# Down projection of three chunks by seven products, with one weight sum per pair made by an accumulating transfer and three by VectorE

## The chip, the core and the metric

The kernel runs on one core of a Trainium2 chip. The metric is the device time of one execution in microseconds (us), as the median of three runs. The profile is one further execution, recorded by the hardware profiler. Engines are called as the profile calls them: PE is TensorE's matmul, DVE is VectorE, ACT is ScalarE, POOL is GpSimd, SP is SyncE, which only issues transfers.

## What is computed

One inference step of an encoder layer over 512 prompt tokens and 64 sample tokens (576 together), width 1024. A mixer and a memory attention come first; the change lies in the last sub-layer, whose reference is

```python
up = rmsnorm(x, g_ffn) @ w_up
a, b = up[..., :D_FF], up[..., D_FF:]
a_ext = jnp.concatenate([conv_hist.astype(a.dtype), a], axis=1)
conv = conv_b + sum(a_ext[:, j:j + T] * conv_w[j] for j in range(CONV_W))
x = x + (jax.nn.silu(conv) * b) @ w_down
```

with D_FF = 2816, and a final RMSNorm behind it. All inputs are fp32.

## The kernel before

Features lie on partitions and the 576 tokens (T) on the free axis, in two halves of 288 (H). A factor of a product is split in two fp32r parts, hi (ACT rounds it) and lo (DVE subtracts hi from the value), and each product of tiles is three matmuls of 128x288: hi by hi, hi by lo, lo by hi.

The 22 hidden tiles f of 128 go in four chunks, `CHUNKS` = (0,4), (4,6), (10,6), (16,6): first the up projection of a chunk's hidden tiles, then the down projection from them into the eight tiles of x_t, the residual. Chunk 0 is plain ("rounds" of f in the code). In chunks 1 to 3, `SLOTS` lists the weight factors in the order in which all engines take them, one slot after the other:

- Up pair e (the columns of a and of b for hidden tile f): seven slots q0 to q6 instead of eight, by a Strassen-like scheme. Factors are w00, s1, s2, w01, s3, s4, w11 (`PRODUCTS`), where s1 to s4 are sums of the four weight blocks, which DVE makes (`slot_sum`, four a pair). A slot is 12 matmuls; q2, q4, q5 and q6 go into a bank whose earlier content has to be taken off first.
- Down pair d (two tiles of x_t): four slots w00, w01, w10, w11 of 18 matmuls. After each second slot DVE adds 576 columns of a finished tile to x_t (L2216).

A factor's way is: SP loads the raw block (`raw_tile`, two buffers raw0 and raw1; the next load into one waits until the last slot of its former holder has been subtracted), ACT rounds it (`slot_high`, L1076), DVE subtracts (`slot_low`, L464), PE multiplies. ACT runs 6 slots ahead of PE (`AHEAD`), DVE 5 slots for the subtraction and 7 for the sums. Each engine works in the order of its program, so an instruction that waits holds up all behind it on its engine.

Between the products of an up pair, DVE takes the results: the gate from q3 and q5 (L2185, L2197), up_b from q4 (L2192), then with ACT's first tap the second and third tap of the convolution (L2052, L2057), and, when ACT has made the silu, the hidden tile (`take_value`, L2165 to L2168). ACT rounds the hidden tile, DVE subtracts (`low_hidden`, part_lo). For hidden tile f this happens while PE is in the slots of pair e + 1. POOL copies the few gate columns that the next tile and the state output need (a_last, conv_hist; L1054, L1058).

For the chunk's last tile nothing of the up projection is left to cover this way: PE begins the down pairs with parts that need only earlier hidden tiles (`down_product` of d = 0 leaves out the last tile's part of its first slots until `hidden_low` is complete).

## Time and profile before

| | us |
|---|---|
| median of 3 runs | 864.05 (863.15 to 865.03) |
| the profiled execution | 863.93 |
| its span, first to last instruction | 862.1 |
| mean granted TensorE clock | 0.998 of full speed |
| PE busy | 828.7 (96%) |
| DVE busy | 605.0 (70%) |
| ACT busy | 437.3 (51%) |
| POOL busy | 142.8 (17%) |

The span holds the work of the engines; the 1.83 us that the execution takes beside it lie before and after. An instruction's duration overlaps with the start of the next one on the same engine, so that the distance from start to start is shorter than the duration, and busy time counts the overlap once.

### The profile page before, as it was taken

Reading aid. Unit: us, or ns where it says so; the run is one execution under the profiler, and the core shown is the slowest. Engines: PE = TensorE matmul, PEld = TensorE weight load, DVE = VectorE, ACT = ScalarE, POOL = GpSimd, SP = SyncE. Lnnn points to the kernel's source line nnn. Section 1 sums busy time; section 2 is a strip of 40 time slices with the busy share of each in tenths; the row PEclk is TensorE's granted clock in tenths of the full one; section 3 lists DMA queues with packets and bytes.
Section 4 is the critical chain, followed back from the end, with each engine's and each line's share of the span. In section 5 each row is a group of like instructions: output and inputs, shape, how many; then the busy total and the mean of one; then the engine's idle time right before and its main releaser. Section 6 shows DMA issues by size and latency. Waiting matters only on the chain.

```text
span 862.1 us, 15501 instructions
## 1 busy us (share of the span) xinstructions
PE 828.7 (96%) x5939; PEld 795.3 (92%) x5939; DVE 605.0 (70%) x1118; ACT 437.3 (51%) x793; POOL 142.8 (17%) x246
## 2 busy tenths in 40 slices
PE   5999999999999999999999999999999999999996
PEld 4798988988997899989998989999999999999995
DVE  3787766677665566554767898998469984699733
ACT  5677666646435554333334444665236652366523
POOL 5015566463000002000000100110001100011100
PEclk9999999999999999999999999999999999999999
DMA  6166434226327533120321323333233323332303
GB/s 215 49 223 169 135 94 113 81 74 233 95 73 284 204 98 122 51 73 2 97 74 50 97 74 100 97 100 110 86 89 89 90 89 95 90 98 86 115 24 111
DMA packets 105141, 91.57 MB, mean 106 GB/s; under 512 B 3008, under 2 KB 96406, under 8 KB 104819
## 3 DMA queue, kind: packets, MB, share of 16 engines
q1 hardware_dynamic: 99939, 73.51, 28.1%
q0 software_dynamic: 5136, 17.17, 6.6%
q8 instruction: 43, 0.70, 0.3%
q14 instruction: 23, 0.19, 0.1%
HBM read 81.32 MB, written 9.35 MB: 105 GB/s over the span
## 4 chain that ended last, share of the span: by engine, by line
PE 80%; DVE 11%; ACT 4%; issue 2%; DMA 2%; SPq 0%; DVEq 0%; ACTq 0%
PE ps L2731 23%; PE ps L434 19%; PE ps L2742 15%; PE ps L2381 4%; PE ps L2274 3%; PE ps L2561 3%; PE ps L2617 2%; PE ps L2567 1%; PE ps L2646 1%; PE ps L2667 1%; DVE w_lo L460 1%; PE ps L2361 1%; DMA x_tok<-in_x_sample 1%; DMA w_raw<-in_w_mk 1%; ACT w_hi L455 1%
## 5 line engine op out<-in xcount | busy, mean ns | idle before, releaser
L2731 PE MATMUL ps<-up_lo,slot_hi 128*128 128x288 f32 x504 | 149.2, 296 | 0.0
L2731 PE MATMUL ps<-up_hi,slot_lo 128*128 128x288 f32 x504 | 148.6, 295 | 0.0
L2731 PE MATMUL ps<-up_hi,slot_hi 128*128 128x288 f32 x504 | 148.5, 295 | 0.0
L1076 ACT ACTIVATE slot_hi<-raw 128x512 fp32r<-128x512 f32 (+2 forms) x118 | 64.6, 554 | 79.9 <-PE ps L2742 55.6
L2731 PEld LDWEIGHTS ps<-up_hi,slot_lo 128*128 128x128 f32 x504 | 95.1, 189 | 0.0
L2731 PEld LDWEIGHTS ps<-up_hi,slot_hi 128*128 128x128 f32 x504 | 95.0, 188 | 0.0
L2731 PEld LDWEIGHTS ps<-up_lo,slot_hi 128*128 128x128 f32 x504 | 94.8, 188 | 0.0
L464 DVE TENSOR_TENSOR slot_lo<-raw,slot_hi 128x512 fp32r<-128x512 f32 (+2 forms) x118 | 70.2, 598 | 31.5 <-ACT slot_hi L1076 31.0
L2742 PE MATMUL ps<-part_hi,slot_hi 128*128 128x288 f32 x352 | 75.5, 295 | 1.9 <-DVE x_t L2216 1.5
L2742 PE MATMUL ps<-part_lo,slot_hi 128*128 128x288 f32 x352 | 75.1, 295 | 0.0
L2742 PE MATMUL ps<-part_hi,slot_lo 128*128 128x288 f32 x352 | 75.0, 294 | 0.0
L1054 POOL COPY a_last<-gate 128x2 f32<-128x2 f32 x44 | 28.1, 668 | 274.3 <-DVE gate L2198 246.3
L434 PE MATMUL ps<-a_hi,w_hi 128*128 128x288 f32 x320 | 69.7, 300 | 2.9 <-DVE w_lo L460 0.9
L460 DVE TENSOR_TENSOR w_lo<-w_raw,w_hi 128x1024 fp32r<-128x1024 f32 x42 | 51.5, 1227 | 24.4 <-ACT w_hi L455 23.8
L434 PE MATMUL ps<-a_lo,w_hi 128*128 128x288 f32 x320 | 68.4, 296 | 0.0
L434 PE MATMUL ps<-a_hi,w_lo 128*128 128x288 f32 x320 | 68.4, 295 | 0.0
L455 ACT ACTIVATE w_hi<-w_raw 128x1024 fp32r<-128x1024 f32 x49 | 51.6, 1053 | 24.1 <-PE ps L434 15.4
L1076 ACT ACTIVATE slot_hi<-row_sum 128x512 fp32r<-128x512 f32 x72 | 45.4, 631 | 36.2 <-PE ps L2731 17.3
L2742 PEld LDWEIGHTS ps<-part_hi,slot_hi 128*128 128x128 f32 x352 | 56.3, 188 | 2.6 <-DVE x_t L2216 2.0
L2742 PEld LDWEIGHTS ps<-part_hi,slot_lo 128*128 128x128 f32 x352 | 56.5, 188 | 0.0
L2742 PEld LDWEIGHTS ps<-part_lo,slot_hi 128*128 128x128 f32 x352 | 56.4, 188 | 0.0
L434 PEld LDWEIGHTS ps<-a_hi,w_hi 128*128 128x128 f32 x320 | 51.4, 189 | 4.5 <-issue 2.5
(408 smaller groups left out, 2078.5 us busy)
## 6 DMA issues: line engine op xcount, KB each, us to landing
raw<-in_w_up SPq DMA_DIRECT2D x36, 512.0 KB, 4.9
raw<-in_w_down SPq DMA_DIRECT2D x12, 768.0 KB, 4.4
w_raw<-in_w_in SPq DMA_DIRECT2D x15, 512.0 KB, 4.1
w_raw<-in_w_o SPq DMA_DIRECT2D x8, 512.0 KB, 4.0
w_raw<-in_w_mq SPq DMA_DIRECT2D x8, 512.0 KB, 4.1
w_raw<-in_w_mo SPq DMA_DIRECT2D x8, 512.0 KB, 4.0
w_raw<-in_w_up SPq DMA_DIRECT2D x8, 512.0 KB, 3.8
w_raw<-in_w_mk SPq DMA_DIRECT2D x6, 512.0 KB, 3.9
```

The costliest lines, as they stand in the source:

```text
L434: mm = nc.tensor.matmul(acc[:, h, 0:H], w[slot][:, c], x[:, k, h * H:h * H + H], start=(k == first and w is w_hi and x is x_hi), stop=(k = ...
L455: nc.scalar.activation(w_hi[slot][:], w_raw[slot][:], ACT.Copy).then_inc(weight_hi_ready, 1)
L460: nc.vector.tensor_tensor(w_lo[slot][:], w_raw[slot][:], w_hi[slot][:].bitcast(F32), ALU.subtract).then_inc(weight_lo_ready, 1)
L464: return nc.vector.tensor_tensor(out, x, hi, ALU.subtract)
L1054: ins = nc.gpsimd.tensor_copy(a_last[:, 2 * g:2 * g + 2, f], gate[:, c:c + 2])
L1076: return nc.scalar.activation(out, x, ACT.Copy, scale=scale)
L2274: ins = mm(b, flat_a[x][:, k * T + t * P:k * T + t * P + P], w[n % 2][:, c], start=(k == 0 and x == 0 and w is w_hi), stop=(k == KT - 1 an ...
L2381: ins = mm(ACC[0][:, half, 0:H], w[n % 2][:, k * P:k * P + P], x[:, k, half * H:half * H + H], start=(k == 0 and w is w_hi and x is a_hi), ...
L2561: ins = mm(banks[t][:, h], x[:, k, t * P:t * P + P], w_hi[slot][:, h * 512:h * 512 + 512], start=(k == 0 and x is mem_hi), stop=False)
L2617: ins = mm(out, flat_b[x][:, col:col + P], kk[:, int(s == SAMPLE), k, :], start=(f == 0 and x == 0 and kk is mk_hi), stop=(f == 1 and x == 1))
L2731: ins = mm(up_bank(k, e, b), w[g % AHEAD][:, m * P:m * P + P], y[:, m, x], start=(first and m == 0 and w is slot_hi and y is up_hi), stop= ...
L2742: ins = mm(acc[:, h, 0:H], w[g % AHEAD][:, m * P:m * P + P], y[:, 2 * m + l, h * H:h * H + H], start=(l == 0 and m == 0 and w is slot_hi a ...
```

## The change

The down pairs of chunks 1 to 3 become seven slots of 9 matmuls instead of four of 18 ("seven" in `SLOTS`). Each slot's result is added to or subtracted from a half (288 columns) of a tile of x_t by DVE as soon as the slot is done (`ADDS`), and PE waits for the addition before it uses the bank again. The hidden tiles are now needed in pairs and as seven factors: DVE makes four mixtures of each two hidden tiles (`mix_hidden`), ACT rounds and DVE subtracts them too (`hidden_mixed_high`, `low_mixed`).

Of the four weight sums of a pair, up pairs and down pairs alike, s1 now comes by transfers: SP loads one block into landed_sum, then POOL adds the other block to it by an accumulating transfer. DVE makes s2, s3, s4. The copies of gate columns move from POOL to ACT. The raw blocks of a down pair are now two transfers; the first four slots of a chunk's down part are (0,0), (0,1), (1,0), (1,1), written (d, q), which need only the even hidden tiles.

The diff, cut:

```diff
-        SUM_HOME = {"s1": 0, "s2": 1, "s3": 2, "s4": 0}
-        SUM_COUNT = {"s1": 1, "s2": 2, "s3": 3, "s4": 4}
+        LANDED_SUM = {"s1": 0}
+        SUM_HOME = {"s2": 0, "s4": 1}
+        SUM_COUNT = {"s2": 1, "s3": 2, "s4": 3}
+        ADDS = [(0, 0, ALU.add), (1, 1, ALU.subtract), (0, 1, ALU.add), (0, 0, ALU.add),
+                (1, 1, ALU.subtract), (0, 1, ALU.add), (1, 0, ALU.subtract)]
+        OPENING = [(0, 0), (0, 1), (1, 0), (1, 1)]
...
+            if k >= 1:
+                order = OPENING + [(d, q) for d in range(DOWN_PAIRS) for q in range(FACTORS) if (d, q) not in OPENING]
+                SLOTS += [("seven", k, d, q, raws + d, PRODUCTS[q][0]) for d, q in order]
...
+                for n in (0, 1) if r == 2 else (r - DOWN_PAIRS,) if r >= DOWN_PAIRS + 2 else ():
+                    if n >= 2:
+                        sp.wait_ge(slot_lo_ready, SUM3[n - 2] + 1)
+                    w, _, seconds = sum_source(n)
+                    sp.dma_start(landed_rows(n, 0), w[0, :, :, seconds]).then_inc(weight_landed[n % 2], 16)
                 raw_tile(r)
...
-                ins.then_inc(edges_copied, 1)
-                if f + 1 < NF:
-                    pool.wait_ge(conv_ready, 2 * f + 2)
-                    nc.gpsimd.tensor_copy(gate[:, GAP:GAP + 2], conv_hist[:, :, f + 1]).then_inc(edges_copied, 1)
...
+                pool.wait_ge(weight_landed[n % 2], PLAIN_LANDED + 16 * (n // 2 + 1))
+                pool.wait_ge(sums_landed[0], SUMS_BEFORE + 16 * n)
+                pool.dma_start(landed_rows(n, 0), w[1, :, :, seconds], accum_op=ALU.add).then_inc(sums_landed[0], 16)
...
+            act.wait_ge(rms_ready, 2)
+            copy(gate[:, GAP:GAP + 2], conv_hist[:, :, 0]).then_inc(edges_copied, 1)
             for f in range(PLAIN - 1):
                 round_weights(act, W_UP + 2 * f + 2, 0, late=True)
...
+            def mix_hidden(f, e):
+                dve.wait_ge(hidden_ready, hidden_parts(f) + 1)
+                x, y = hidden_of(f), hidden_of(f + 1)
+                if e % 2 == 0:
+                    minus(hidden_mixed[:, 0], x[:, 0:H], x[:, H:T]).then_inc(hidden_ready, 1)
+                    return
+                link.inc(nc.vector.scalar_tensor_tensor(hidden_mixed[:, 1], hidden_mixed[:, 0], -1.0, x[:, H:T], mult, sub))
+                minus(hidden_mixed[:, 2], x[:, H:T], y[:, H:T])
+                dve.wait_ge(dve_link, link.now)
+                nc.vector.scalar_tensor_tensor(hidden_mixed[:, 3], hidden_mixed[:, 1], -1.0, x[:, 0:H], mult,
+                                               sub).then_inc(hidden_ready, 1)
...
+                elif kind == "seven":
+                    if (e, q) == (0, 0):
+                        low_hidden(f0 + nf - 1, nf - 1)
+                    dve.wait_ge(slot_used, g + 1)
+                    i, j, op = ADDS[q]
+                    x = x_t[:, 2 * e + i, j * H:j * H + H]
+                    nc.vector.tensor_tensor(x, x, seven_bank(e, PRODUCTS[q][2]), op).then_inc(down_taken, 1)
+                    if (e, q) == (0, 0):
+                        low_mixed(f0 + nf - 1, nf - 1)
+                    slot_sum(g + AHEAD + 1)
...
+                    if q in (2, 4, 5, 6):
+                        added(e, {2: 0, 4: 2, 5: 1, 6: 4}[q])
```

Three places show how the order of instructions moves. The first is DVE where a chunk passes from its up part to its down part. The rows begin with the third tap of the chunk's last hidden tile. Before, from there to the first addition to x_t:

```order
L2057 SCALAR_TENSOR_TENSOR conv_a<-gate,conv_par,conv_b 128x578 [waits conv_ready]
L464 TENSOR_TENSOR slot_lo_167<-raw_176,slot_hi_165 128x384 [waits slot_hi_ready]
L2165 SCALAR_TENSOR_TENSOR hidden<-ps,silu 128x288 [waits hidden_low,slot_used,hidden_hi,silu_ready]
L2167 SCALAR_TENSOR_TENSOR hidden<-up_b,silu 128x224 [waits up_taken]
L2168 SCALAR_TENSOR_TENSOR hidden<-up_b,silu 128x64
L464 TENSOR_TENSOR slot_lo_168<-raw_176,slot_hi_166 128x384 [waits slot_hi_ready]
L464 TENSOR_TENSOR part_lo<-hidden,part_hi 128x576 [waits hidden_hi,hidden_ready]
L464 TENSOR_TENSOR slot_lo_183<-raw_176,slot_hi_179 128x384 [waits slot_hi_ready]
L464 TENSOR_TENSOR slot_lo_184<-raw_176,slot_hi_180 128x384 [waits slot_hi_ready]
L2216 TENSOR_TENSOR x_t<-x_t,ps 128x576 [waits slot_used]
```

After, the same place from the mixtures on, which stand right behind the hidden tile, to the addition of slot (0,1) (hidden_180 is the odd, hidden_160 the even tile; seven_lo holds the lo parts of the factors that come from hidden tiles):

```order
L2177 SCALAR_TENSOR_TENSOR hidden_mixed<-hidden_mixed,hidden_180 128x288 [waits hidden_ready]
L475 TENSOR_TENSOR hidden_mixed<-hidden_180,hidden_160 128x288
L2180 SCALAR_TENSOR_TENSOR hidden_mixed<-hidden_mixed,hidden_180 128x288 [waits dve_link]
L2138 TENSOR_TENSOR landed_sum_177<-raw_163 128x384 [waits slot_lo_ready]
L475 TENSOR_TENSOR slot_lo_167<-raw_163,slot_hi_165 128x384 [waits slot_hi_ready]
L475 TENSOR_TENSOR seven_lo<-hidden_180,seven_hi 128x576 [waits hidden_hi]
L2337 TENSOR_TENSOR x_t<-x_t,ps 128x288 [waits slot_used]
L475 TENSOR_TENSOR seven_lo<-hidden_mixed,seven_hi 128x864 [waits hidden_hi]
L2138 TENSOR_TENSOR row_sum_162<-row_sum_161,raw_163 128x384 [waits row_sums,slot_lo_ready]
L475 TENSOR_TENSOR slot_lo_188<-landed_sum_177,slot_hi_184 128x384 [waits slot_hi_ready]
L2337 TENSOR_TENSOR x_t<-x_t,ps 128x288 [waits slot_used]
```

What moved: the addition of slot (0,0), for which PE's slot (0,2) waits, stands behind three mixtures, a sum, a weight subtraction and the 128x576 subtraction. Behind these rows come, up to the addition of slot (0,2), for which PE's slot (0,4) waits: subtraction and addition for (1,0), a sum, subtraction and addition for (1,1), and subtraction and addition for (0,2) itself.

The second is DVE inside the up part, in the slots q2 to q4 of a pair that follows an odd hidden tile. After:

```order
L475 TENSOR_TENSOR slot_lo_187<-raw_181,slot_hi_183 128x512 [waits slot_hi_ready]
L2177 SCALAR_TENSOR_TENSOR hidden_mixed<-hidden_mixed,hidden_180 128x288 [waits hidden_ready]
L475 TENSOR_TENSOR hidden_mixed<-hidden_180,hidden_160 128x288
L2180 SCALAR_TENSOR_TENSOR hidden_mixed<-hidden_mixed,hidden_180 128x288 [waits dve_link]
L2138 TENSOR_TENSOR row_sum_161<-landed_sum_178,raw_181 128x512 [waits slot_lo_ready,row_sums,cache_k_landed,raw_landed1]
L475 TENSOR_TENSOR slot_lo_166<-landed_sum_178,slot_hi_164 128x512 [waits slot_hi_ready]
L2307 TENSOR_TENSOR gate<-snap_157,ps 128x288 [waits conv_ready,edges_copied,snapped,slot_used]
L475 TENSOR_TENSOR seven_lo<-hidden_180,seven_hi 128x576 [waits hidden_hi]
L475 TENSOR_TENSOR slot_lo_167<-row_sum_161,slot_hi_165 128x512 [waits slot_hi_ready]
L2313 TENSOR_TENSOR up_b<-snap_158,ps 128x288 [waits snapped,slot_used]
L475 TENSOR_TENSOR seven_lo<-hidden_mixed,seven_hi 128x864 [waits hidden_hi]
L2138 TENSOR_TENSOR landed_sum_178<-raw_181 128x512 [waits slot_lo_ready]
```

What moved: before, the same stretch holds no mixture and no 128x864 subtraction; it has the sum of s1 (in q1) more.

The third is ACT at the start of the up projection of chunk 0, where the weights of the third column block are rounded (w_hi). Before:

```order
L1337 ACTIVATE inv_rms<-ps,eps 128x576 [waits mean_done]
L1453 ACT_TABLE_LOAD
L1453 ACTIVATE stat<-stat 128x1
L455 ACTIVATE w_hi_51<-w_raw_49 128x1024 [waits weight_used,weight_landed0]
L1468 ACTIVATE conv_a<-gate,conv_par 128x578 [waits edges_copied,acc_free]
L1474 ACTIVATE silu<-conv_a 128x578 [waits hidden_ready,conv_ready]
```

After:

```order
L1407 ACTIVATE inv_rms<-ps,eps 128x576 [waits mean_done]
L1523 ACT_TABLE_LOAD
L1523 ACTIVATE stat<-stat 128x1
L1146 ACTIVATE gate<-conv_hist 128x2 [waits rms_ready]
L466 ACTIVATE w_hi_51<-w_raw_49 128x1024 [waits weight_used,weight_landed0]
L1540 ACTIVATE conv_a<-gate,conv_par 128x578 [waits edges_copied,acc_free]
L1146 ACTIVATE a_last<-gate 128x2 x2
L1551 ACTIVATE silu<-conv_a 128x578 [waits conv_ready]
```

What moved: the copy of conv_hist, formerly POOL's, stands ahead of the rounding on ACT and waits for rms_ready, which DVE gives when inv_rms is complete.

## Rows read from the trace of the kernel before

**Rows 1.** Page, part 1: busy us, share of the span, instructions.
```profile
PE 828.7 (96%) x5939; PEld 795.3 (92%) x5939; DVE 605.0 (70%) x1118; ACT 437.3 (51%) x793; POOL 142.8 (17%) x246
```
**Rows 2.** Chain that ended last: start us, length us, what.
```profile
639.09 66.77 PE ps L2731 x504
705.86 38.03 PE ps L2742 x288
743.90 66.77 PE ps L2731 x504
...
848.96 0.77 DVE x_t L2216
```
**Rows 3.** Windows, chunk 2's up and down part: length, then PE, PEld, DVE, ACT, POOL.
```profile
639.09:705.86 66.77, 66.77 (x507) 66.77 (x506) 60.19 (x117) 42.09 (x76) 9.85 (x17) 1.00 0.32 91
705.86:743.90 38.04, 38.04 (x291) 38.04 (x290) 20.14 (x34) 10.10 (x18) 0.45 (x1) 1.00 0.31 92
```
**Rows 4.** Timeline of DVE in one up pair: start us, duration us, instruction, wait ahead.
```profile
652.82 0.69 DVE L464 TENSOR_TENSOR slot_lo<-raw,slot_hi 128x512 fp32r<-128x512 f32 x1 [0.34 <-ACT slot_hi L1076]
...
654.23 0.69 DVE L2042 TENSOR_TENSOR row_sum<-raw 128x512 f32<-128x512 f32 x1
654.83 0.69 DVE L464 TENSOR_TENSOR slot_lo<-raw,slot_hi 128x512 fp32r<-128x512 f32 x1
...
656.64 0.45 DVE L2185 TENSOR_TENSOR gate<-snap,ps 128x288 f32<-128x288 f32 x1
657.00 0.76 DVE L464 TENSOR_TENSOR part_lo<-hidden,part_hi 128x576 fp32r<-128x576 f32 x1
657.67 0.69 DVE L464 TENSOR_TENSOR slot_lo<-row_sum,slot_hi 128x512 fp32r<-128x512 f32 x1
...
663.93 0.69 DVE L464 TENSOR_TENSOR slot_lo<-raw,slot_hi 128x512 fp32r<-128x512 f32 x1 [0.30 <-ACT slot_hi L1076]
```
**Rows 5.** Timeline of DVE at the end of chunk 2's up part.
```profile
697.34 0.69 DVE L464 TENSOR_TENSOR slot_lo<-raw,slot_hi 128x512 fp32r<-128x512 f32 x1 [0.33 <-ACT slot_hi L1076]
...
704.31 0.39 DVE L2197 TENSOR_TENSOR gate<-snap,ps 128x224 f32<-128x224 f32 x1 [0.50 <-PE ps L2731]
704.62 0.22 DVE L2198 TENSOR_TENSOR gate<-snap,ps 128x64 f32<-128x64 f32 x1
705.78 0.82 DVE L2052 SCALAR_TENSOR_TENSOR conv_b<-gate,conv_par,conv_a 128x578 f32<-128x578 f32 x1 [0.94 <-ACT conv_a L1468]
706.63 0.82 DVE L2057 SCALAR_TENSOR_TENSOR conv_a<-gate,conv_par,conv_b 128x578 f32<-128x578 f32 x1
707.37 0.55 DVE L464 TENSOR_TENSOR slot_lo<-raw,slot_hi 128x384 fp32r<-128x384 f32 x1
708.21 0.46 DVE L2165 SCALAR_TENSOR_TENSOR hidden<-ps,silu 128x288 f32<-128x288 f32 x1 [0.28 <-ACT silu L1474]
...
709.02 0.55 DVE L464 TENSOR_TENSOR slot_lo<-raw,slot_hi 128x384 fp32r<-128x384 f32 x1
709.92 0.76 DVE L464 TENSOR_TENSOR part_lo<-hidden,part_hi 128x576 fp32r<-128x576 f32 x1 [0.35 <-ACT part_hi L1076]
```
**Rows 6.** Timeline of DVE in chunk 0's down part: a subtraction of 1152 columns.
```profile
514.40 1.35 DVE L464 TENSOR_TENSOR up_lo<-mixed,up_hi 128x1152 fp32r<-128x1152 f32 x1
515.67 0.42 DVE L464 TENSOR_TENSOR slot_lo<-raw,slot_hi 128x256 fp32r<-128x256 f32 x1
```
**Rows 7.** Timeline of DVE at the start of the up projection.
```profile
460.30 3.75 DVE L1908 RECIPROCAL inv_rms<-inv_rms 128x576 f32<-128x576 f32 x1 [2.89 <-ACT inv_rms L1337]
464.09 1.23 DVE L460 TENSOR_TENSOR w_lo<-w_raw,w_hi 128x1024 fp32r<-128x1024 f32 x1
```
**Rows 8.** Timeline of ACT there.
```profile
461.58 0.20 ACT L1453 ACTIVATE stat<-stat 128x1 f32<-128x1 f32 x1
461.69 1.04 ACT L455 ACTIVATE w_hi<-w_raw 128x1024 fp32r<-128x1024 f32 x1
```
**Rows 9.** Timeline of PE there.
```profile
466.17 0.54 PE L434 MATMUL ps<-a_hi,w_hi 128*128 128x288 f32 x2 [0.30 <-DVE gate L2114]
```
**Rows 10.** Transfers by line: times issued, KB each, median us to landing.
```profile
raw<-in_w_down SPq DMA_DIRECT2D x12, 768.0 KB, 4.4
...
kc_raw<-in_cache_fox_k POOLq DMA_DIRECT2D x4, 512.0 KB, 5.5
...
wp_raw<-in_w_pool POOLq DMA_DIRECT2D x1, 256.0 KB, 3.4
```

More of the change, by code:

```diff
@@ L298, in build @@
         snap = [place(f"snap{c}", [P, H]) for c in range(3)]
-        hidden = place("hidden", [P, T])
-        row_sum = [place(f"row_sum{s}", [P, 4 * P]) for s in range(3)]
+        hidden = [place("hidden0", [P, T])]
+        row_sum = [place(f"row_sum{s}", [P, 4 * P]) for s in range(2)]
         tile_raw = [place("raw0", [P, KT, 2 * P])]
@@ L314, in build @@
         assert here[0] <= at["part_lo"]
+        here[0] = at["whole"]
+        hidden_mixed = place("hidden_mixed", [P, 4, H])
+        assert here[0] <= at["conv_tok"]
+        here[0] = at["part_hi"]
+        seven_hi = place("seven_hi", [P, 3, FACTORS, H], F32R)
+        assert here[0] <= at["up_lo"]
+        here[0] = at["a_hi"]
+        landed_sum = [place(f"landed_sum{c}", [P, 2, 4 * P]) for c in range(2)]
+        seven_lo = place("seven_lo", [P, 3, FACTORS, H], F32R)
+        hidden.append(place("hidden1", [P, T]))
+        assert here[0] <= at["b_hi"]
         here[0] = at["w_raw0"]
@@ L1545, in _ @@
                         whole_high(m)
-                if kind == "down" and f0 + nf == NF and (e, q) == (2, 0):
+                if kind == "seven" and f0 + nf == NF and (e, q) == (3, 0):
                     act.wait_ge(y_turned, 1)
-                    copy(conv_tok[:], ps[2][0:4 * NF, 0, 0:P]).then_inc(conv_tok_ready, 1)
+                    copy(conv_tok[:], ps[0][0:4 * NF, 0, 0:P]).then_inc(conv_tok_ready, 1)
             nc.scalar.activation(stat[:, 62:63], stat[:, 61:62], ACT.Sqrt)
@@ L2140, in _ @@
                 dve.wait_ge(silu_ready, f + 1)
-                nc.vector.tensor_tensor(hidden[:, 0:TP], silu[:, 0:TP], up_b[:, 0:TP], mult)
-                nc.vector.tensor_tensor(hidden[:, TP:T], silu[:, GAP:GAP + TS], up_b[:, TP:T], mult).then_inc(hidden_ready, 1)
+                nc.vector.tensor_tensor(hidden_of(f)[:, 0:TP], silu[:, 0:TP], up_b[:, 0:TP], mult)
+                nc.vector.tensor_tensor(hidden_of(f)[:, TP:T], silu[:, GAP:GAP + TS], up_b[:, TP:T], mult).then_inc(hidden_ready, 1)
                 if f == 3:
@@ L2180, in _ @@
                         take_value(k, e - 1, g - 2)
+                    if q == 2 and e > 0:
+                        mix_hidden(f - 1, e - 1)
                     if q == 3:
@@ L2746, in down_product, with seven_product @@
                     ins.then_inc(slot_used, 1)
+            def seven_product(g, d, q, tiles):
+                _, x, b = PRODUCTS[q]
+                first = q in (0, 1, 3)
+                for m in tiles:
+                    for w, y in ((slot_hi, seven_hi), (slot_hi, seven_lo), (slot_lo, seven_hi)):
+                        ins = mm(seven_bank(d, b), w[g % AHEAD][:, m * P:m * P + P], y[:, m, x],
+                                 start=(first and m == 0 and w is slot_hi and y is seven_hi),
+                                 stop=(m == 2 and w is slot_lo), skip_group_check=not first)
+                if tiles[-1] == 2:
+                    ins.then_inc(slot_used, 1)
```

232 lines of the change are left out of this document (163 added, 69 removed).

## Prediction

> **What bounds the kernel now.** I read the page first: PE is busy 96% of the span, DVE 70%, ACT 51% [rows 1]. That is an average, so I went to the chain that ended last. From chunk 1's up part to the end of chunk 3's down part it is PE alone, without a gap: chunk 2's up part is 504 matmuls in 66.77 us, its down part 288 in 38.03 us [rows 2], which is 132.5 and 132.0 ns from one matmul to the next. Every matmul taken out there is worth 0.132 us as long as PE stays fed. Who might fail to feed it is told by the windows by stage: in the up part DVE is busy 60.2 of 66.8 us, in the down part only 20.1 of 38.0 [rows 3]. DVE's timeline then shows that even the 60.2 is an average. Within one steady up pair, from 652.82 to 663.93 us, it stands still for only 0.3 us of 11.1 [rows 4], and PE needs 7 x 12 x 0.1325 = 11.13 us for the pair. So PE and DVE are within a few per cent of each other in the up part, and the change gives DVE work.
>
> **DVE's prices.** Instructions follow each other more closely than their durations say. A 512-column operation lasts 0.69 us, and the next starts 0.60 later; 288 columns 0.36, 576 columns 0.67 [rows 4], 1152 columns 1.27 [rows 6]. Between these I take 0.46 for 384 (it lasts 0.55, which is 0.14 less than 512 [rows 5]) and 0.97 for 864. An addition of 288 from PSUM lasts 0.45, and PE sees it about 0.05 later. The Trainium skill, VectorE: DVE Perf Modes, section on the TRN2 errata, gives an fp32 tensor_tensor (N+151)/0.96 ns, 691 ns for 512: the durations here agree, the distances do not. By the page's figure the 18 operations of the passage below would cost 18 x 0.09 us more in each chunk, 4.9 us in all, and the sum would be 878.6; the start times are measured, so I go by them.
>
> **Matmuls.** Each of 12 down pairs has 7 x 9 = 63 instead of 72: 108 less, x 0.132 = **-14.3 us**, 4.76 a chunk.
>
> **The passage from up to down part.** Let T be the end of PE's last up product (705.86 in chunk 2). Before, the gate is added at T-1.55, the taps and the silu follow, and the hidden tile's three parts, begun at 708.21, are through by 709.1, T+3.2 [rows 5]. This chain is the same after. Behind it DVE now does in order: three mixtures (3 x 0.36), s3 (0.46), a weight subtraction (0.46), the 576 subtraction (0.67): T+6.0. Only then the addition of (0,0), which PE sees at T+6.5. PE has four slots that need nothing of the last tile, 4 x 9 x 0.1325 = 4.76 us, and its fifth, (0,2), waits for that addition: **1.7 us**. DVE goes on: 864 subtraction (T+7.3), s4 (7.8), subtraction and addition for (0,1) (8.6), the same for (1,0) (9.4), s2 (9.9), the same for (1,1) (10.7) and (0,2) (11.5, seen at 11.65). PE does (0,2) and (0,3) by T+8.9, and (0,4) waits for the addition of (0,2): **2.75 us**. A last **0.2** falls on (0,6). From pair d = 1 on DVE needs 7 x 0.82 + 3 x 0.46 = 7.1 us a pair against PE's 8.3, and stays ahead. ACT's work (half busy) lies beside this. Together 4.7 a chunk, about what the products save there.
>
> The passage also begins late. The raw block of d = 1 is now needed for the third slot of the down part, not for the fifth, so ACT, 6 slots ahead, asks for it at the end of q3, T-4.77. Its buffer is free when DVE has subtracted the up part's last slot, before at 697.34 + 0.69, T-7.8 [rows 5]; 768 KB take 4.4 us [rows 10], so T-3.4 at best. ACT rounds it by T-2.9 (0.52 us), and behind that DVE has a subtraction, up_b, a mixture's subtraction, s2 and a subtraction (2.1 us) before it comes to the gate: T-0.75 instead of T-1.55, 0.8 late if DVE is on time. It is not (below), so I take **1.15** for the delay, and **0.8** more that PE waits in q6 for up_b. Bounds: 0 and 2.
>
> **The up part.** Two pairs lose two sums (-1.2) and get four mixtures (+1.44), a mixed subtraction of 288 and one of 864 (+1.33); the hidden tiles' own subtractions go from 2 x 0.67 to 0.36 + 0.67 (-0.31). That is +1.26, so 10.7 us a pair become 10.5 in pairs behind an even tile and 12.3 behind an odd one, 11.4 in the mean, over PE's 11.13. The first pair of a chunk has no hidden tile to work on (7.9 us), so DVE enters on time. PE feels a delay where q6 needs DVE's up_b: DVE has it some 0.4 us after q4 when on time, PE asks 1.59 us after q4. Carried forward slot by slot with these prices, with the wait for ACT at each q1, that addition ends 0.4, 1.3, 1.8 and 2.5 us after q4 in pairs 1 to 4: 0.2 and 0.9 too late in pairs 3 and 4. **1.1 us** a chunk; bounds 0 (ordering absorbs it) and 2.
>
> **ACT's new wait.** At the start of the up projection, w_hi is rounded at 461.69 us [rows 8], while DVE still makes the reciprocal of inv_rms until 464.05, and DVE's w_lo follows at 464.09 [rows 7]. Now ACT first waits for that reciprocal: a small copy (0.20 like the 128x1 [rows 8]) overlapped with the rounding of 1.04 puts w_lo at about 465.35, and the gate behind it too. PE already waited 0.30 us for that gate [rows 9], and a chain of DVE and ACT hangs on it. **+1.25**; 0 to 1.5. The other copies that ACT takes over fall where it waits for the taps.
>
> **The end.** The last addition has 288 columns instead of 576, whose row is 0.77 [rows 2]: **-0.3**.
>
> **Transfers.** An s1 has to come through SP's load and then POOL's accumulating transfer. Within the up part some ten slots (16 us) are open for it: hidden. The tight one is d = 1 again: its buffer is free when s3 of the chunk's last up pair is subtracted, five slots ahead of PE, at the end of the pair before (T-11.1 and DVE 1.5 late: T-9.6), and ACT wants it behind the late raw block, at about T-2.2. No row shows an accumulating transfer. 192 KB can hardly be faster than 3.4 (256 KB from POOL) and hardly slower than 5.5 (512 KB, since the sum moves its destination twice) [rows 10]. With 3.4 for the load, 0.6 for POOL's issue and 3.4 to 5.5 it lands at T-2.2 to T-0.1: nothing, or up to 1.5 us a chunk. I take nothing, since it is a plain 192 KB and nearer to the first.
>
> **Sum.** Per chunk -4.76 + 4.65 + 1.15 + 0.8 + 1.1 = +2.95; three chunks +8.8; +1.25 - 0.3: +9.8 on the profiled execution's 863.93, **873.7 us**, slower. (That execution is 0.1 below the median.)
>
> **Rivals.**
> *No change.* Only the order of the passage holds, and DVE keeps time elsewhere: -14.3 + 14.0 + 1.25 - 0.3 = +0.7, 864.6. For it: the price list of the up part is over PE's by 2% only. Against: 697.34's block lands late whatever DVE does.
> *Faster.* The passage is shorter than I count: its additions come on time, for instance because ACT and DVE reach the last tile earlier than before. It decides below (14.3 - 0.95)/3 = 4.4 us of waiting a chunk; without any the time is 850.6, with half of the 4.65 and none elsewhere 857.6. For it: DVE is idle for half of the old down part [rows 3]. Against: that idleness lies behind the passage, not in it, and DVE works in order.
> *Slower still.* The accumulating transfers land late at d = 1: +1.5 a chunk, 878.2; it decides from 3.4 us upwards. The Trainium skill, DMA: Bandwidth & Descriptors, section on the anatomy of one DMA, gives 2.0 us + bytes/436e3, 2.45 us for 192 KB, by which it would be in time; no run here shows it.
>
> **Chances.** A measurement of this kernel can tell about 0.2%, 1.7 us. My forecast (866 to 877) 0.60, later still 0.13, no change 0.14, faster 0.13. So slower 0.73, same 0.14, faster 0.13. The range, 863.5 to 879, leaves out the faster case and the tail of the late transfers, nearly 2 in 10; the forecast's own is 866 to 877.
>
> **What would show it.** In the profile after: PE's waits, which were none in these chunks, name x_t's addition three times, with two long ones, 1.7 to 3 and 2.5 to 3 us, in each passage; waits for up_b before q6 in the later pairs; the down part of a chunk near 38 us as before although it has 252 matmuls instead of 288; the w_hi rounding behind the reciprocal. The prediction is wrong if the passage's waits are under 4.4 us a chunk, if DVE's new operations are closer than I priced them, or if the accumulating transfers are much slower than any row.

## The result and the profile after

The changed kernel takes 880.24 us (median of 4 runs, 877.98 to 883.67) against 864.09 for the kernel before: a ratio of **1.019 (95% interval 1.0155 to 1.0226)**, slower. Timed again, with five runs on the chip of three of the experiments, it took 878.45 against 863.17, 1.0181 (1.0167 to 1.0195). The forecast was 873.7 with a range up to 879: the direction was right, the loss was 16.2 us by the medians instead of 9.8, and the time lies above the range. The execution profiled after is the fastest of its four, 877.98 us, 14.05 above the one of before and just inside the range.

Part 1 of the page, after (columns as in [rows 1]):

```profile
PE 823.3 (94%) x5831; PEld 786.2 (90%) x5831; DVE 666.6 (76%) x1286; ACT 466.7 (53%) x913; POOL 146.8 (17%) x210
```

108 matmuls fewer, and 61.6 us more of DVE. The windows of chunk 2's up and down part, after (columns as in [rows 3]):

```profile
644.67:714.36 69.69, 67.54 (x506) 66.88 (x506) 63.93 (x128) 43.54 (x96) 7.64 (x6) 1.00 0.55 126
714.36:753.64 39.28, 35.70 (x254) 34.96 (x254) 36.71 (x79) 18.06 (x35) 5.13 (x4) 0.96 0.58 137
```

The windows begin as in [rows 3], 0.16 us behind the start of a part's first matmul. Both parts are longer than the 66.77 and 38.04 of [rows 3]: the up part by 2.9 us with the same products, the down part by 1.2 with an eighth fewer. In chunk 1 they grew by 3.3 and 2.2, in chunk 3 by 3.1 and 1.4. Together that is 14.1 us, and the whole loss. Before, PE stood nowhere in these stretches [rows 2]; the three largest waits of PE from the up projection on, after (waited for, total us, times, longest us):

```profile
PE ps L2884 <- DVE x_t L2337: 11.6, 6, 2.8
PE ps L2862 <- DVE up_b L2313: 6.8, 8, 1.7
PE ps L445 <- DVE gate L2234: 1.6, 1, 1.6
```

L2862 is the up product, L2884 the new down product. Where these waits stand in chunk 2 is told by PE's timeline (start us, duration us, instruction, idle ahead of it and who ended it):

```profile
687.83 0.37 PE L2862 MATMUL ps<-up_hi,slot_hi 128*128 128x288 f32 x1 [0.16 <-DVE up_b L2313]
699.76 0.37 PE L2862 MATMUL ps<-up_hi,slot_hi 128*128 128x288 f32 x1 [0.56 <-DVE up_b L2313]
712.54 0.37 PE L2862 MATMUL ps<-up_hi,slot_hi 128*128 128x288 f32 x1 [1.43 <-DVE up_b L2313]
721.65 0.40 PE L2884 MATMUL ps<-seven_hi,slot_hi 128*128 128x288 f32 x1 [2.52 <-DVE x_t L2337]
726.90 0.40 PE L2884 MATMUL ps<-seven_hi,slot_hi 128*128 128x288 f32 x1 [1.06 <-DVE x_t L2337]
```

The first three are q6 of the up pairs e = 3, 4 and 5, the last two are (0,2) and (0,4). The up part ends at T = 714.36, so (0,2) starts at T+7.3 and (0,4) at T+12.5. What DVE does behind the up part's last slot (answers to [rows 5]):

```profile
705.41 0.69 DVE L475 TENSOR_TENSOR slot_lo<-raw,slot_hi 128x512 fp32r<-128x512 f32 x1
...
711.47 0.56 DVE L475 TENSOR_TENSOR slot_lo<-raw,slot_hi 128x384 fp32r<-128x384 f32 x1 [2.29 <-ACT slot_hi L1146]
711.95 0.45 DVE L2313 TENSOR_TENSOR up_b<-snap,ps 128x288 f32<-128x288 f32 x1
...
713.62 0.38 DVE L2320 TENSOR_TENSOR gate<-snap,ps 128x224 f32<-128x224 f32 x1
...
721.15 0.45 DVE L2337 TENSOR_TENSOR x_t<-x_t,ps 128x288 f32<-128x288 f32 x1
721.52 1.05 DVE L475 TENSOR_TENSOR seven_lo<-hidden_mixed,seven_hi 128x864 fp32r<-128x864 f32 x1
```

and ACT's two roundings for the second down pair in the same place:

```profile
710.91 0.52 ACT L1146 ACTIVATE slot_hi<-raw 128x384 fp32r<-128x384 f32 x1 [2.86 <-DMA raw<-in_w_down]
711.99 0.52 ACT L1146 ACTIVATE slot_hi<-landed_sum 128x384 fp32r<-128x384 f32 x1 [0.22 <-DMA landed_sum<-in_w_down]
```

The reader is to see one chain: the block of d = 1 can be loaded only once its buffer's last subtraction is done (706.1), lands at 710.9, and up_b stands behind it in DVE's order, so PE waits for up_b at 712.54; DVE waited 2.29 us there and comes late to the passage: the gate is added at T-0.7 instead of T-1.55. The accumulated sum is 0.22 late for ACT, and DVE does not stand for it. In chunk 3 it is later, and DVE does:

```profile
822.04 0.52 ACT L1146 ACTIVATE slot_hi<-landed_sum 128x384 fp32r<-128x384 f32 x1 [1.13 <-DMA landed_sum<-in_w_down]
822.60 0.56 DVE L475 TENSOR_TENSOR slot_lo<-landed_sum,slot_hi 128x384 fp32r<-128x384 f32 x1 [0.23 <-ACT slot_hi L1146]
```

The chain that ended last leads through this transfer in chunks 2 and 3. In chunk 2 that is a coincidence of times, since up_b starts 0.48 us behind the start of the subtraction ahead of it, as in the other chunks; in chunk 3 it is worth the 0.23 us.

The transfers, after (times issued, KB each, median us from issue to landing; answers to [rows 10]):

```profile
landed_sum<-in_w_down SPq DMA_DIRECT2D x12, 192.0 KB, 2.6
landed_sum<-in_w_down POOLq DMA_DIRECT2D x12, 192.0 KB, 5.5
```

At the start of the up projection ACT's copy waits 2.31 us for the reciprocal, and w_hi follows it (answers to [rows 8]; PE's wait for the gate is the third row of the waits above, 1.6 us against 0.30 in [rows 9]):

```profile
462.95 0.20 ACT L1146 ACTIVATE gate<-conv_hist 128x2 f32<-128x2 f32 x1 [2.31 <-DVE inv_rms L2004]
463.06 1.04 ACT L466 ACTIVATE w_hi<-w_raw 128x1024 fp32r<-128x1024 f32 x1
```

Last, the granted clock (windows: length, then busy of PE, PEld, DVE, ACT, POOL, the granted clock, DMA share, GB/s):

```profile
716.00:721.00 5.00, 3.14 (x24) 2.91 (x22) 4.68 (x11) 3.22 (x6) 0.00 (x0) 1.00 0.00 0
721.00:727.00 6.00, 4.28 (x19) 3.96 (x19) 6.00 (x14) 1.87 (x4) 0.43 (x1) 0.72 0.14 41
```

and in chunk 1, for PE alone (length, busy, granted clock, DMA share, GB/s):

```profile
612.00:616.00 4.00, 3.28 (x18) 0.63 0.17 49
616.00:620.00 4.00, 3.08 (x13) 0.52 0.89 218
620.00:624.00 4.00, 4.00 (x32) 1.00 0.54 117
```

Behind the first wait of the passage the clock falls for 3 to 7 us to its lower level (0.50, 1.2 GHz, matmuls 0.24 us apart). In chunks 2 and 3 it is back before the second wait ends. In chunk 1 it comes back at 619.9, 2.9 us behind the start of (0,4) at 616.92.

### The profile page after: what moved, and what is told of

It reads as the page before. It is cut to its first block, busy times and chain, and to the rows that moved or that the text cites. A ratio compares the mean times of both kernels' runs of the same rounds, so it can differ in the third digit from the quotient of the medians.

```text
span 876.1 us, 15733 instructions
## 1 busy us (share of the span) xinstructions
PE 823.3 (94%) x5831; PEld 786.2 (90%) x5831; DVE 666.6 (76%) x1286; ACT 466.7 (53%) x913; POOL 146.8 (17%) x210
## 4 chain that ended last, share of the span: by engine, by line
PE 59%; DVE 26%; ACT 6%; DMA 4%; issue 4%; SPq 0%; DVEq 0%; ACTq 0%
PE ps L445 19%; PE ps L2884 9%; PE ps L2862 7%; DVE slot_lo L475 5%; PE ps L2512 4%; PE ps L2692 3%; PE ps L2405 3%; DMA landed_sum<-in_w_down 2%; DVE row_sum L2138 2%; PE ps L2748 2%; DVE seven_lo L475 2%; PE ps L2873 1%; PE ps L2698 1%; DVE conv_b L2148 1%; PE ps L2777 1%
## 5 line engine op out<-in xcount | busy, mean ns | idle before, releaser
L2862 PE MATMUL ps<-up_hi,slot_hi 128*128 128x288 f32 x504 | 149.2, 296 | 6.9 <-DVE up_b L2313 6.8
L2862 PE MATMUL ps<-up_lo,slot_hi 128*128 128x288 f32 x504 | 149.1, 296 | 0.0
L2862 PE MATMUL ps<-up_hi,slot_lo 128*128 128x288 f32 x504 | 148.4, 294 | 0.0
L2862 PEld LDWEIGHTS ps<-up_hi,slot_hi 128*128 128x128 f32 x504 | 94.8, 188 | 8.9 <-DVE slot_lo L475 7.7
L2862 PEld LDWEIGHTS ps<-up_hi,slot_lo 128*128 128x128 f32 x504 | 95.0, 188 | 0.0
L2862 PEld LDWEIGHTS ps<-up_lo,slot_hi 128*128 128x128 f32 x504 | 94.7, 188 | 0.0
L2884 PE MATMUL ps<-seven_hi,slot_hi 128*128 128x288 f32 x252 | 77.7, 308 | 11.6 <-DVE x_t L2337 11.6
L1128 POOL DMA_DIRECT2D landed_sum<-in_w_up x18 | 23.1, 1284 | 344.7 <-issue 183.5
L1146 ACT ACTIVATE slot_hi<-raw 128x512 fp32r<-128x512 f32 (+2 forms) x106 | 58.1, 555 | 36.2 <-PE ps L2884 16.9
L475 DVE TENSOR_TENSOR slot_lo<-raw,slot_hi 128x512 fp32r<-128x512 f32 (+2 forms) x106 | 63.5, 603 | 17.6 <-ACT slot_hi L1146 16.4
L2884 PE MATMUL ps<-seven_lo,slot_hi 128*128 128x288 f32 x252 | 76.8, 305 | 0.0
L2884 PE MATMUL ps<-seven_hi,slot_lo 128*128 128x288 f32 x252 | 76.7, 304 | 0.0
L2884 PEld LDWEIGHTS ps<-seven_hi,slot_hi 128*128 128x128 f32 x252 | 49.5, 197 | 13.6 <-DVE x_t L2337 13.5
L1146 ACT ACTIVATE slot_hi<-landed_sum 128x512 fp32r<-128x512 f32 (+1 forms) x60 | 35.2, 587 | 40.8 <-DVE landed_sum L2138 23.8
L1146 ACT ACTIVATE slot_hi<-row_sum 128x512 fp32r<-128x512 f32 (+1 forms) x60 | 35.2, 587 | 37.2 <-DVE row_sum L2138 22.5
L445 PEld LDWEIGHTS ps<-a_hi,w_lo 128*128 128x128 f32 x320 | 51.5, 189 | 0.0
```

The lines of the kernel that those rows point to most:

```text
L445: mm = nc.tensor.matmul(acc[:, h, 0:H], w[slot][:, c], x[:, k, h * H:h * H + H], start=(k == first and w is w_hi and x is x_hi), stop=(k = ...
L475: return nc.vector.tensor_tensor(out, x, hi, ALU.subtract)
L1128: pool.dma_start(landed_rows(n, 0), w[1, :, :, seconds], accum_op=ALU.add).then_inc(sums_landed[0], 16)
L1146: return nc.scalar.activation(out, x, ACT.Copy, scale=scale)
L2862: ins = mm(up_bank(k, e, b), w[g % AHEAD][:, m * P:m * P + P], y[:, m, x], start=(first and m == 0 and w is slot_hi and y is up_hi), stop= ...
L2884: ins = mm(seven_bank(d, b), w[g % AHEAD][:, m * P:m * P + P], y[:, m, x], start=(first and m == 0 and w is slot_hi and y is seven_hi), st ...
```

## Experiments

All are edits of the changed kernel. Each ratio is against the kernel before on the same chip; the changed kernel's own is 1.0181 to 1.019.

**1. The control.** 

> The changed kernel as it is, on the chip of the next three, for comparison: 1.019 of the kernel before, as measured, with a spread of runs of a few microseconds.

Measured 878.45 us, 1.0181 (1.0167 to 1.0195). Its profile has the same waits in each chunk, within 0.6 us.

**2. s1 made by DVE again.**

```diff
-        LANDED_SUM = {"s1": 0}
+        LANDED_SUM = {}
-        SUM_COUNT = {"s2": 1, "s3": 2, "s4": 3}
+        SUM_COUNT = {"s1": 1, "s2": 2, "s3": 3, "s4": 4}
...
-                    sp.dma_start(landed_rows(n, 0), w[0, :, :, seconds]).then_inc(weight_landed[n % 2], 16)
...
-                pool.dma_start(landed_rows(n, 0), w[1, :, :, seconds], accum_op=ALU.add).then_inc(sums_landed[0], 16)
```

> The changed kernel with one part undone: DVE makes all four weight sums of a pair again, and neither the load nor the accumulating transfer of s1 exists. Theory A (DVE's load sets the pace of the up part): an up pair gets 0.60 us of DVE work more, so the waits of PE for up_b before q6 appear from the second pair on and add up to about 3 us more in each chunk; some 889 us. Theory B (what is late is the accumulated sum, or the software transfers slow the loads): the waits for up_b shrink and the time falls to 877 or below. If the transfers cost nothing and DVE has room, it stays at 880.

Measured 883.98 us, 1.0242 (1.0228 to 1.0255). PE's waits, this run:

```profile
PE ps L2874 <- DVE x_t L2327: 14.2, 6, 2.6
PE ps L2852 <- DVE up_b L2303: 10.8, 12, 1.6
```

Twelve waits for up_b instead of eight, 10.8 us instead of 6.8: DVE's load sets the pace of the up part, as theory A has it, and the accumulating transfer is a gain. The size is half of what I expected (about 5 us, not 9), because the wait in the last pair, which is that for the late block, doesn't grow (1.41 in chunk 2, 1.43 before).

**3. s3 by transfer too.**

```diff
-        LANDED_SUM = {"s1": 0}
+        LANDED_SUM = {"s1": 0, "s3": 1}
...
+                    sp.dma_start(landed_rows(n, 1), w[0, :, :, firsts]).then_inc(weight_landed[n % 2], 16)
...
+                pool.dma_start(landed_rows(n, 1), w[0, :, :, seconds], accum_op=ALU.add).then_inc(sums_landed[1], 16)
```

> The changed kernel with s3 made by a second load and a second accumulating transfer too, so that DVE makes two sums of a pair and not three. Theory A (DVE's load): an up pair has 0.60 us less of DVE work, the waits for up_b in the third to fifth pair vanish and only the one behind the late raw block stays (about 1.2 us a chunk); s3 no longer stands ahead of the addition of (0,0), so the wait before (0,2) is 0.46 shorter; together about 2 us a chunk, 874 us. Theory B (transfers): two accumulating transfers of 6.5 us in series and an issue of 1.28 us each on POOL make s3 late, above all for the second down pair; 882 or more.

Measured 871.86 us, 1.0108 (1.0093 to 1.0122). PE's waits:

```profile
PE ps L2886 <- DVE x_t L2339: 11.8, 6, 2.6
PE ps L2864 <- DVE up_b L2315: 2.5, 3, 0.9
```

Theory A: only one wait for up_b is left in each chunk, the one behind the block, and it is 0.7 to 0.9 us instead of 1.4 to 1.7. The wait before (0,2) is 2.0 us in chunks 1 and 3, where it was 2.5 and 2.8. In chunk 2 it stays at 2.5: there DVE stood 0.39 us for the rounding of an accumulated sum.

**4. DVE's order in the passage.**

```diff
+        FIRST_ADDS = [(0, 0), (0, 2), (0, 1), (0, 4), (1, 0), (0, 3), (0, 5), (1, 1), (0, 6)]
...
                     if q == 5 and e == nf - 1:
+                        slot_sum(g + 8)
+                        slot_sum(g + 9)
                         second_tap(f)
                         third_tap(f)
                     if q == 6 and e == nf - 1:
                         take_value(k, e, g)
                         mix_hidden(f, e)
-                    slot_sum(g + AHEAD + 1)
+                        add_product(k, 0, 0)
...
+                    if s == 0:
+                        low_hidden(f0 + nf - 1, nf - 1)
+                        slot_low(g + AHEAD - 1)
+                        low_mixed(f0 + nf - 1, nf - 1)
+                        continue
```

> The changed kernel with DVE's order in the passage alone changed: s3 and s4 of the first down pair are made while DVE waits for ACT ahead of the taps, the addition of (0,0) stands right behind the mixtures, the subtraction of 864 right behind the hidden tile's, and the addition of (0,2) ahead of those of (0,1), (1,0) and (1,1). The same operations in all. Theory A (the passage's loss is one of order): PE's waits before (0,2) and (0,4), 4.5 us a chunk, become about 1.7, the granted clock stays up for longer, and the time falls by 8 to 10 us to about 871. Theory B (DVE simply has too much to do there): the waits move to the products behind, as waits for weight subtractions, and the time stays within 2 us of 880.

Measured 877.16 us, 1.0157 (1.0141 to 1.0172): a gain of about 2 us, not 8 to 10. PE's timeline in chunk 2:

```profile
720.39 0.41 PE L2909 MATMUL ps<-seven_hi,slot_hi 128*128 128x288 f32 x1 [0.85 <-DVE x_t L2301]
...
731.94 0.61 PE L2909 MATMUL ps<-seven_hi,slot_hi 128*128 128x288 f32 x1 [1.96 <-DVE x_t L2301]
```

The waits before (0,2) and (0,4) shrink from 3.6 to 0.9, and a new one of 1.96 stands before (1,4), five products behind (0,4). Behind it the clock is at 0.50 for 3.4 us in chunks 1 and 2, which takes back a part of the gain. In chunk 1 the chain leads from that wait back through the third down pair's accumulating transfer, so I took the sum for late.

**5. The sums loaded earlier on top of that.**

```diff
-                        sp.wait_ge(slot_lo_ready, SUM3[n - 2] + 1)
+                        sp.wait_ge(slot_lo_ready, SLOT_OF[SLOTS[SUM3[n - 2]][0:3] + (1,)] + 1)
+                        sp.wait_ge(row_sums, 3 * (n - 2) + 1)
```

> DVE's new order in the passage as in the run before (additions first), and the load of s1 two pairs on starts when s1 of its buffer has been subtracted and s2 made from it, instead of when s3 has been subtracted: about 10 us earlier. Theory A (with the new order the loss is only one of the accumulated sum that lands late: load 2.6 us and accumulating transfer 5.6 us behind s3's subtraction, seen in the third down pair with a wait of 2.0 us): that wait goes, about 2.2 us in each chunk against the new order alone, some 7 us, so 1.008 of the kernel before. Theory B (DVE is the limit there whatever lands): the wait stays, 1.015.

Measured 876.00 us, 1.0149 (1.0135 to 1.0163). PE's timeline in chunk 1:

```profile
622.09 0.40 PE L2910 MATMUL ps<-seven_hi,slot_hi 128*128 128x288 f32 x1 [1.93 <-DVE x_t L2302]
```

The wait stays, 1.93 us: theory A fell, the sum was not what PE waited for. The addition that ends it is DVE's tenth of the passage, that of (1,2), which my order had put behind those of (1,1) and (0,6), for which no product waits so soon. What did change is the clock: behind the same waits the down parts of chunks 1 and 2 are 1.6 us shorter than in experiment 4, with the clock at 1.00. In chunk 3 a raw block came late, the wait was 3.16 us, the clock stood at 0.50 for 5.9 us behind it, and the down part is 3.3 us longer.

**6. The late block, shortened.**

```diff
+                    if kind == "seven" and i == 1:
+                        rows, w = 2, w[0:2 * P, :]
                     sp.dma_start(tile_raw[r % 2][:, 0:rows, half * P:half * P + P],
```

> The changed kernel, in which the raw block of the second down pair (d = 1) of each chunk is transferred by a third only (two of its six row tiles; that part of the weights is left out, so the output is not the reference's), which lets it land about 2 us earlier; every instruction stays. Theory A (the passage begins late because this block lands late): DVE's wait of 2.3 us for ACT's rounding of it goes, the wait of PE before q6 of the last pair falls from 1.4 to 1.7 us to about 0.6, and the passage's addition of (0,0) comes about 0.9 us earlier; 1.8 us a chunk, about 874.5. Theory B (DVE is behind anyway by its load): the wait moves and the time stays at 879 to 880.

Measured 874.07 us, 1.0125 (1.0107 to 1.0143), 5 us less. PE's waits:

```profile
PE ps L2886 <- DVE x_t L2339: 13.0, 6, 4.1
PE ps L2864 <- DVE up_b L2315: 2.2, 6, 0.6
```

The long wait in each last pair (1.4 to 1.7 us) is gone, and no wait for up_b is over 0.6: theory A. But one wait before (0,2) has grown to 4.1. It stands in chunk 3, and DVE's timeline there names the accumulated sum, which is now the later of the two:

```profile
818.94 0.56 DVE L475 TENSOR_TENSOR slot_lo<-landed_sum,slot_hi 128x384 fp32r<-128x384 f32 x1 [1.97 <-ACT slot_hi L1148]
```

In chunk 2 DVE stands 0.33 us for it, in chunk 1 not at all.

**7. PE kept busy in the first wait.**

```diff
+                    if (e, q) == (0, 2):
+                        for _ in range(18):
+                            mm(ps[3][:, 1, H:512], seven_hi[:, 0, H00, 0:P], seven_hi[:, 0, H00, 0:512 - H],
+                               start=True, stop=True, skip_group_check=True)
                     if q in (2, 4, 5, 6):
```

> The changed kernel with 18 matmuls of 224 columns more in each passage, into columns that nobody reads, which PE runs where it otherwise waits for the addition of (0,0); about 2.0 us of the 2.5 to 2.8 that it stands still. Theory A (the fall of the granted clock to its lower level behind that wait costs time of its own): the clock stays at 1.00 through the passage, the products behind the second wait run at 0.132 us a matmul, and 1.3 us or more of chunk 1 and less of the others come back: 1 to 4 us in all. Theory B (the slow matmuls lie within the wait for DVE that follows): no difference within 1 us.

Measured 878.44 us, 1.0187 (1.0167 to 1.0208): no difference. PE's timeline in chunk 1, and windows of PE (length, busy, granted clock, DMA share, GB/s) in chunk 3:

```profile
611.88 0.40 PE L2884 MATMUL ps<-seven_hi,slot_hi 128*128 128x288 f32 x1 [0.46 <-DVE x_t L2337]
617.12 0.40 PE L2884 MATMUL ps<-seven_hi,slot_hi 128*128 128x288 f32 x1 [2.60 <-DVE x_t L2337]
```

```profile
830.00:835.00 5.00, 2.64 (x18) 0.98 0.15 39
835.00:841.00 6.00, 5.64 (x33) 0.73 0.84 197
```

(0,2) now follows 0.46 us of standing still, but it and (0,4) start no earlier: PE then waits 2.6 us for the addition of (0,2) instead of 1.1 to 1.7. So matmuls at the lower level between the two waits cost nothing here (theory B). In chunks 1 and 2 the clock stayed at 1.00; in chunk 3 it fell behind the second wait, where it does cost: 33 matmuls in 5.64 us, against 4.37 at 0.1325.

**8. ACT's copy behind the first rounding.**

```diff
-            act.wait_ge(rms_ready, 2)
-            copy(gate[:, GAP:GAP + 2], conv_hist[:, :, 0]).then_inc(edges_copied, 1)
             for f in range(PLAIN - 1):
                 round_weights(act, W_UP + 2 * f + 2, 0, late=True)
+                if f == 0:
+                    act.wait_ge(rms_ready, 2)
+                    copy(gate[:, GAP:GAP + 2], conv_hist[:, :, 0]).then_inc(edges_copied, 1)
```

> The changed kernel with one part moved: ACT waits for the reciprocal of inv_rms and makes its first small copy behind the first rounding of weights of the up projection, not ahead of it. Theory A (ACT's wait ahead of that rounding delays w_lo and so PE's first gate): PE's wait for the gate falls from 1.6 to 0.3 us and the time by about 1.25 us, 1.0165 of the kernel before. Theory B (the delay is absorbed before the up part begins): no change, 1.018.

Measured 877.04 us, 1.0149 (1.0133 to 1.0164). PE's timeline there:

```profile
464.74 0.53 PE L445 MATMUL ps<-a_hi,w_hi 128*128 128x288 f32 x2 [0.30 <-DVE gate L2235]
```

The wait is 0.30 as in [rows 9], and chunk 1's up part begins at 532.74 against 534.32: theory A. From the start of the reciprocal to this product it takes 5.87 us, as before the change; in the changed kernel it is 7.14. The gain in time reads as 3 us, which is more than the wait; part of it lies within the spread of the runs.

**9. Transfers, order and wait together.** s1 and s3 landed, each loaded when its own buffer is free, the block in two halves with a semaphore and a wait each, the order of experiment 4, ACT's wait of experiment 8; the core of what is new:

```diff
+                    if r - 2 >= DOWN_PAIRS and half == 0:
+                        sp.wait_ge(row_sums, 2 * (r - 2 - DOWN_PAIRS) + 2)
+                        sp.wait_ge(slot_lo_ready, SLOT_OF[SLOTS[FIRST_OF_RAW[r - 2]][0:3] + (3,)] + 1)
+                    if r - 2 >= DOWN_PAIRS and half == 1:
+                        sp.wait_ge(slot_lo_ready, LAST_OF_RAW[r - 2] + 1)
```

> All that helped, together: both sums that the transfers can make (s1 and s3) landed, their loads started as soon as their buffers are free, the raw block's two halves freed and waited for apart (the first half about 4 us earlier), DVE's new order in the passage, and ACT's wait for the reciprocal moved behind the first rounding. If the losses are those named (DVE's work in the up part, the order of the passage, the late block, late sums, ACT's wait) and add up, about 1.5 us a chunk of waiting is left, and the time is about 856, 0.992 of the kernel before. If the software transfers or DVE's total work set the pace, it stays above 1.000.

Measured 858.04 us, **0.9938 (0.9925 to 0.9952)**, 0.6% faster than the kernel before. No wait for up_b is left; PE's waits:

```profile
PE ps L2929 <- DVE x_t L2321: 4.4, 5, 1.4
```

**10. The same with the changed kernel's order.** Experiment 9 without `FIRST_ADDS` and what hangs on it.

> As the run of everything together, but with the changed kernel's own order of DVE's work in the passage: both sums landed and loaded early, the block's halves apart, ACT's wait moved. Theory A (the order is a loss of its own): the two waits before (0,2) and (0,4) come back, about 4 us a chunk less the 1.4 that stood there, so some 8 us on 858: 866, 1.003 of the kernel before. Theory B (the order costs only as long as the block and the sums are late): under 860, 0.996.

Measured 865.57 us, 1.0029 (1.0017 to 1.0041). PE's timeline in chunk 2 is the passage by itself, with nothing late ahead of it:

```profile
710.85 0.40 PE L2904 MATMUL ps<-seven_hi,slot_hi 128*128 128x288 f32 x1 [1.31 <-DVE x_t L2357]
716.09 0.61 PE L2904 MATMUL ps<-seven_hi,slot_hi 128*128 128x288 f32 x1 [2.60 <-DVE x_t L2357]
```

Theory A: the order alone turns the gain of 0.6% into a loss of 0.3%. A part of that comes by the clock. The down parts take 37.8, 39.3 and 40.7 us with the same waits; behind the second wait the clock is at 1.00 in chunk 1, at 0.50 for 3.1 us in chunk 2 and for 6.2 us in chunk 3 (PE there: length, busy, granted clock, DMA share, GB/s):

```profile
822.00:829.00 7.00, 6.76 (x30) 0.54 0.97 213
```

**11. A second order.** Shown against experiment 9.

```diff
-        FIRST_ADDS = [(0, 0), (0, 2), (0, 1), (0, 4), (1, 0), (0, 3), (0, 5), (1, 1), (0, 6)]
+        FIRST_ADDS = [(0, 0), (0, 2), (0, 1), (0, 4), (1, 0), (0, 3), (0, 5), (1, 2), (1, 1), (1, 4), (1, 3), (0, 6)]
```

> Everything together, and the additions of (1,2) and (1,4) placed ahead of (1,1), (1,3) and (0,6), for which no product waits so soon. Theory A (the wait of 1.4 us in each chunk that is left is one of DVE's order too): it goes, about 4 us, 854, 0.989 of the kernel before. Theory B (DVE's backlog of the passage has to be paid somewhere): the wait moves to a later product, 858, 0.994.

Measured 856.20 us, **0.9920 (0.9906 to 0.9934)**. PE's waits, and the windows of chunk 2's up and down part:

```profile
PE ps L2931 <- DVE x_t L2321: 2.5, 10, 0.3
```

```profile
635.36:702.25 66.89, 66.89 (x507) 66.89 (x506) 61.09 (x124) 44.89 (x98) 15.72 (x13) 1.00 0.88 181
702.25:738.27 36.02, 35.01 (x254) 33.70 (x254) 33.89 (x74) 16.43 (x34) 9.70 (x8) 1.00 0.87 192
```

The waits of 1.4 us are gone, ten of 0.15 to 0.34 have come: theory A, at less than half its size (1.6 us by the ratios, not 4). The up part runs without a wait, as before the change, and the down part is 2.0 us shorter than in [rows 3]; the products alone would save 4.76. Of the 2.7 us between, PE's timeline has 2.5 at six stops: four with the listed waits, 0.9 us together, and two that are too short to be listed.

**12. No accumulation.**

```diff
-                pool.dma_start(landed_rows(n, 0), w[1, :, :, seconds], accum_op=ALU.add).then_inc(sums_landed[0], 16)
+                pool.dma_start(landed_rows(n, 0), w[1, :, :, seconds]).then_inc(sums_landed[0], 16)
```

> The changed kernel in which POOL's transfer overwrites its destination instead of adding to it (the second block of s1 stays, the first is left out, so the output is not the reference's). Theory A (the accumulation is what makes the transfer slow): 192 KB land in about 3.4 us instead of 5.5, like the plain one of 256 KB from POOL. Theory B (the software queue is slow for this layout in any case): 5 us or more. The time stays near 878 in both, since the transfer is mostly hidden.

One run, 881.00 us. The transfers:

```profile
landed_sum<-in_w_down SPq DMA_DIRECT2D x12, 192.0 KB, 2.6
landed_sum<-in_w_down POOLq DMA_DIRECT2D x12, 192.0 KB, 4.8
```

Between the theories: 4.8 us without the accumulation, 5.5 with it, in the same order of loads. But neither is a fixed price. In experiment 5, where the load and the accumulating transfer start earlier, the latter lands sooner than the plain one here:

```profile
landed_sum<-in_w_down POOLq DMA_DIRECT2D x12, 192.0 KB, 4.0
```

So where the transfer stands among the others changed it by more than the addition did. What of the rest is POOL's and what the layout's, no run tells.

## Why the prediction was right in direction, and where it fell short

**Matmuls, -14.3.** Right: experiment 11, with nearly all waits gone, has the same products, and lies 7.3 us under the kernel before on its chip; its chunk 2 is 1.9 us shorter than in [rows 3], with what the small stops leave of the 4.76.

**The passage, 4.65 a chunk and 1.15 for its late start.** The mechanism and the timetable were right: (0,2) was forecast at T+7.65 and (0,4) at T+12.8; they start at T+7.3 and T+12.5 in chunks 1 and 2, at T+7.6 and T+12.9 in chunk 3. The late start was 0.8 in chunks 1 and 2, and 1.1 in chunk 3. Experiment 10 shows the passage without the late start, and without s3 on DVE: waits of 1.3 and 2.6, forecast 1.7, less 0.46 for s3, and 2.75. The 0.2 before (0,6) did not appear. What was too small is the rest. I let the 22 products behind the second wait run at 0.132 from the first matmul on, 26.1 us; chunk 2 took 26.74 and chunk 1 27.75, in which the clock stayed at its lower level until 2.9 us behind the wait. So the down part lost 6.9, 6.0 and 6.2 us against its 252 matmuls at the pace of before (about 33.3), not 5.8: 1.7 us in all.

**The up part, 1.1, and the wait in q6 of the last pair, 0.8.** Here is the step that failed: 1.9 us a chunk forecast, 3.3, 2.9 and 3.1 measured, 3.6 us in all. Experiment 6 separates the two terms. With the late block out of the way its up parts are 1.2 to 1.3 us longer than before the change; this is DVE's load by itself, forecast as 1.1. The rest, 1.6 to 2.0 us a chunk, is PE's wait for up_b in q6 of the last pair, forecast as 0.8: this term was mis-sized, and makes 3.1 of the 5.3 us that the forecast lacked in the three chunks. The wait was larger because the two causes add up: DVE, behind by its load, gave the buffer free at 706.1, 6.6 ahead of the end that the part would have had without this stop (I had 7.8), and the load took 4.8 where I had 4.4. Each stop also costs PE about 0.24 more than it stands still (2.15 us idle in chunk 2, 2.92 lost). Experiment 6 takes away this wait alone; experiment 3 takes away those of the other pairs and half of this one. So both causes are shown, and that they add.

**ACT's new wait, +1.25.** Right: from the start of the reciprocal to PE's product on the gate it is 7.14 us, before 5.87, and experiment 8 gives it back. In the profiled execution it doesn't show in the time, since that was 1.1 us earlier ahead of this place (the reciprocal starts at 459.17, before at 460.30 [rows 7]). In the profiled runs of the changed kernel and its edits this start lies between 458.7 and 460.4, so such a difference is one of executions.

**The end, -0.3.** Right: the last addition of 288 columns lasts 0.46, against 0.77 in [rows 2].

**The transfers, 0.** Nearly right for this order. The sum lands 0.2 to 0.3 us late for ACT behind a later block in chunks 1 and 2, without DVE standing for it, and 1.1 late in chunk 3, where it costs 0.23 us; 5.5 us is the upper end of my bounds, not the lower one that I had taken for nearer. The rival that they delay a chunk was masked by the late block, not wrong in kind: with the block out of the way, in experiment 6, DVE stands 1.97 us for the sum in chunk 3. Its other side, that taking s1 off DVE is worth something, is shown by experiments 2 and 3.

**The sum.** 9.8 forecast and 5.3 more in the three chunks (3.1 for the wait in q6, 0.5 for the load, 1.7 for the down part), less the 1.1 of the earlier start: 14.0, measured 14.05. The median of the first four runs lies 2.3 us above this execution; the kernel's runs spread over 6 us, those of the kernel before over 2. The traces show one cause that can do this. In the runs with the changed kernel's order of additions, the 22 products behind the second wait take 26.4 to 26.8 us where the clock is back before them, 27.7 to 28.2 where it is at 0.50 for 2.9 to 3.4 us of them, and 29.4 with 6.2 us. The slowest of the four runs has a mean granted clock of 0.985, the others 0.990 to 0.992. That this makes the whole spread is likely, but not shown. The range ended at 879 because I gave the late transfers the only tail; the wait in q6 and the clock had none.

**The rival "faster"** named its point, 4.4 us of waiting a chunk, and that is about where experiment 10 stands: 3.9 us of waits in the passage, and with what the stops and the clock cost beyond that 1.0029. Its condition, that the additions come on time, doesn't hold in DVE's written order and does hold in experiment 11's.
